# Three transformer blocks in one program: another way to sum the experts, another place for the overflow code, another order of waits at the head

## The chip, the core and the metric

One core of a Trainium2 chip. The time is that of the device for one execution, in microseconds: 2055.23 us, median of 3 runs (2053.47 to 2059.28). TensorE multiplies, ScalarE and VectorE work on rows of up to 128 partitions, GpSimd does small preparations, SyncE issues the stream of weights.

## The reference

Three blocks over 256 tokens of width 1024, all in float32. The one in which most of the change lies is the expert layer of the second block:

```python
logits = xt @ router_w                      # 256 x 8
top_val, top_idx = lax.top_k(logits, 2)
gates = softmax(top_val)
# each token goes to its 2 experts:
y[e] = (silu(x_e @ w1[e]) * (x_e @ w3[e])) @ w2[e]
h = h + sum over the two experts of gate * y[e]
```

Before it come gated linear attention, windowed attention, block attention, differential attention, a dense SwiGLU of width 2816 and a spatial gating unit; behind it a gated embedding layer ("ple"), then the third block (two attentions and a dense SwiGLU) and a last norm.

## The kernel before

All weights of the dense products come in 1 MB chunks (128 x 2048 floats), in the order of use, through a ring of three slots (`stream_part`, two DMAs of half a chunk each). ScalarE rounds each half to a reduced format (`split_high`, L235), VectorE subtracts that from the raw one (`split_low`, L244), and TensorE makes each product from three matmuls, high by high, high by low, low by high (`times`, L259 to L261). A slot of the ring is free when VectorE is through; a slot of the split parts when TensorE is (`used`). ScalarE and VectorE split two chunks ahead of TensorE (`AHEAD`). Everything on an engine runs in program order; there is no planner.

`gated_pe`, `gated_act` and `gated_dve` are the SwiGLU loop for one expert or one dense layer: a turn of the loop takes three chunks, two of up-projection (24 matmuls of 256 columns) and one of down-projection (12 of 512). Each has a hook `between(n)`: n = 0 stands between the two first up-projections, n = 1 before the last down-projection.

The experts run one after the other, each over 128 slots. `route_*` finds the gates and a place for each token in each expert, and a flag `more` that says whether one expert got more than 128 tokens. A 0/1 matrix (`choose`) gathers an expert's tokens by matmul (`gather`, L2575). Before the first expert VectorE also makes 16 matrices of gate-weighted selections (L2665), TensorE transposes them (L2584) and ScalarE copies them to `spread` (L2633). Each expert's sums are copied to `outs` (L2642). At the end TensorE multiplies `spread` by `outs` in plain float32, 32 matmuls, token tile by token tile (L2611), and VectorE adds each quarter to `h` (L2688). Two chunks of zeros follow the experts in the stream, so that what the loop splits ahead is nothing that is used.

Then every engine reads the flag into a register (`overflow`, L2694) and jumps over the code for a second round of experts, which lies in the middle of the program, if the flag is 0, as it is for these inputs. SyncE does the same before it goes on with the stream.

At the head (`block1_*`) all engines wait for three loads issued by ScalarE: the identity, the columns of gains and `gla_down`. TensorE transposes the first half of h's columns (`turn_first`), and in `first_products` waits for all of chunk 0 before it transposes the rest and multiplies. `down_pe` multiplies by `gla_down`'s parts behind that. ScalarE and VectorE meanwhile scale the transposed columns to `xT`, split chunk 0 and 1 and find the norm (`deferred_act`, `scale_h_dve`). The same functions, without the loads, stand at the start of each layer.

## Time and profile before

| what | value |
|---|---|
| median of 3 runs | 2055.23 us |
| the profiled execution | 2054.95 us |
| its span | 2053.5 us |
| TensorE busy | 1941.5 us, 95% |
| VectorE busy | 1399.5 us, 68% |
| ScalarE busy | 1224.5 us, 60% |
| read from memory | 448.95 MB |

The span is the time between the first and last instruction that the profiler saw. PE is TensorE's matmul, PEld its weight load, which overlaps; DVE is VectorE, ACT ScalarE, SP SyncE, POOL GpSimd; a q behind the name is the engine's own queue of control instructions and DMA issues. Matmuls are pipelined, so the length of one in a timeline is longer than the distance to the next. L12 is line 12 of the kernel.

### The profile page before, as it was taken

To read this page: it belongs to the slowest core of one execution; us is meant where nothing else is said; L and a number is where in the kernel's file an instruction comes from. 1 tells how busy PE (TensorE), PEld (TensorE's weight loads), DVE (VectorE), ACT (ScalarE), POOL (GpSimd) and SP (SyncE) were. 2 spreads that over 40 slices of the span, in tenths; PEclk is the share of its full clock that TensorE was granted. 3 is DMA by queue.
4 is the path that set the end of the run, shared out by engine and by line. 5 is a ranking of instruction groups with operands and counts; after the bars stand their busy time and mean duration, and the time that the engine had idled before them with its cause. 6 is when DMAs were issued, how large, how long until landed. Compare 5 with 4: busy or idle time off the path is not lost.

```text
span 2053.5 us, 38415 instructions
## 1 busy us (share of the span) xinstructions
PE 1941.5 (95%) x13371; PEld 1742.7 (85%) x13371; DVE 1399.5 (68%) x2160; ACT 1224.5 (60%) x2091; POOL 48.0 (2%) x85
## 2 busy tenths in 40 slices
PE   7989889899999989999999999999999798999997
PEld 6859789799989878888889888889897697879997
DVE  4565566754556778888888888888886465655445
ACT  6535455444456567777777777777775465445444
POOL 1000000000000000000000000000000021200000
PEclk9979999999999989999999999999999899999999
DMA  7516243455546549898989898989997242225552
GB/s 272 181 62 213 95 141 118 137 182 179 179 145 208 165 148 350 314 343 313 350 308 353 305 345 305 346 314 351 324 344 288 99 158 81 66 86 171 182 178 89
DMA packets 128854, 451.24 MB, mean 220 GB/s; under 512 B 15118, under 2 KB 20142, under 8 KB 128512
## 3 DMA queue, kind: packets, MB, share of 16 engines
q1 hardware_dynamic: 120496, 437.83, 61.7%
q10 hardware_dynamic: 8272, 12.25, 1.8%
q8 instruction: 55, 0.90, 0.2%
q14 instruction: 31, 0.25, 0.0%
HBM read 448.95 MB, written 4.22 MB: 221 GB/s over the span
## 4 chain that ended last, share of the span: by engine, by line
PE 69%; DVE 12%; issue 8%; ACT 8%; DMA 3%; ACTq 0%; DVEq 0%; SPq 0%
PE ps L259 20%; PE ps L260 19%; PE ps L261 19%; DVE low L244 5%; ACT high L235 4%; DMA ring<-in_stream 3%; PE ps L1015 2%; PE ps L998 1%; PE ps L2611 1%; DVE work L745 1%; PE ps L2575 1%; PE ps L393 1%; PE ps L919 1%; PE ps L655 1%; DVE xT_low L2657 1%
## 5 line engine op out<-in xcount | busy, mean ns | idle before, releaser
L244 DVE TENSOR_TENSOR low<-ring,high 128x1024 fp32r<-128x1024 f32 x832 | 984.8, 1222 | 248.4 <-ACT high L235 244.6
L259 PE MATMUL ps<-high,xT_high 128*128 128x256 f32 (+1 forms) x3256 | 961.4, 295 | 24.6 <-DVE xT_low L325 13.2
L235 ACT CAST high<-ring 128x1024 fp32r<-128x1024 f32 x832 | 840.2, 1054 | 180.9 <-PE ps L261 164.2
L260 PE MATMUL ps<-low,xT_high 128*128 128x256 f32 (+1 forms) x3256 | 941.4, 289 | 0.0
L261 PE MATMUL ps<-high,xT_low 128*128 128x256 f32 (+1 forms) x3256 | 937.8, 288 | 0.0
L259 PEld LDWEIGHTS ps<-high,xT_high 128*128 128x128 f32 x3256 | 615.6, 189 | 47.5 <-DVE xT_low L325 15.4
L260 PEld LDWEIGHTS ps<-low,xT_high 128*128 128x128 f32 x3256 | 617.4, 190 | 12.2
L261 PEld LDWEIGHTS ps<-high,xT_low 128*128 128x128 f32 x3256 | 615.5, 189 | 9.7
L259 PE MATMUL ps<-high,smallT_high 128*128 128x512 f32 (+2 forms) x582 | 243.7, 419 | 10.8 <-DVE smallT_low L750 6.2
L261 PE MATMUL ps<-high,smallT_low 128*128 128x512 f32 (+2 forms) x582 | 226.4, 389 | 0.0
L260 PE MATMUL ps<-low,smallT_high 128*128 128x512 f32 (+2 forms) x582 | 225.9, 388 | 0.0
L259 PEld LDWEIGHTS ps<-high,smallT_high 128*128 128x128 f32 (+1 forms) x582 | 110.7, 190 | 61.7 <-DVE smallT_low L750 43.9
L745 DVE TENSOR_TENSOR work<-ps,work 128x128 f32<-128x128 f32 (+1 forms) x220 | 68.4, 311 | 113.4 <-ACT work L707 111.1
L261 PEld LDWEIGHTS ps<-high,smallT_low 128*128 128x128 f32 (+1 forms) x582 | 110.8, 190 | 24.1
L260 PEld LDWEIGHTS ps<-low,smallT_high 128*128 128x128 f32 (+1 forms) x582 | 111.7, 192 | 16.0
L704 ACT ACTIVATE work<-ps 128x128 f32<-128x128 f32 x176 | 49.1, 279 | 112.0 <-PE ps L261 112.0
L707 ACT ACTIVATE work<-ps,small 128x128 f32<-128x128 f32 x88 | 27.6, 364 | 143.0 <-PE ps L261 142.9
L1044 ACT ACTIVATE logit<-logit,small 128x128 f32<-128x128 f32 (+1 forms) x80 | 36.2, 454 | 102.6 <-DVE small L1077 75.7
L655 PE MATMUL ps<-consts,work 128*128 128x128 f32 x264 | 65.0, 274 | 8.7 <-DVE work L745 8.7
L750 DVE TENSOR_TENSOR smallT_low<-ps,smallT_high 128x128 fp32r<-128x128 f32 (+1 forms) x220 | 68.4, 311 | 6.1 <-ACT smallT_high L712 5.2
L712 ACT CAST smallT_high<-ps 128x128 fp32r<-128x128 f32 (+1 forms) x220 | 62.9, 286 | 12.7 <-PE ps L655 7.5
L1222 ACT ACTIVATE proj<-ps,small 128x256 f32<-128x256 f32 x82 | 34.3, 470 | 51.4 <-PE ps L261 51.3
(329 smaller groups left out, 1171.6 us busy)
## 6 DMA issues: line engine op xcount, KB each, us to landing
ring<-in_stream SPq DMA_DIRECT2D x832, 512.0 KB, 5.5
bias_rows<-bias_line ACTq DMA_DIRECT2D x2, 1536.0 KB, 14.3
wide<-in_wide_rows ACTq DMA_DIRECT2D x5, 512.0 KB, 5.4
work<-bias_rows ACTq DMA_DIRECT2D x2, 1024.0 KB, 11.0
h<-in_x SPq DMA_DIRECT2D x2, 512.0 KB, 4.9
work<-bias_rows ACTq DMA_DIRECT2D x2, 512.0 KB, 6.7
consts<-in_consts ACTq DMA_DIRECT2D x1, 869.0 KB
work<-in_p ACTq DMA_DIRECT2D x2, 256.0 KB, 3.2
```

What stands on the lines that cost most here:

```text
L235: A.e.copy(k.high[:, slot, cols], k.ring[:, slot, cols]).then_inc(flow.high_made, 1)
L244: V.e.tensor_tensor(k.low[:, slot, cols], k.ring[:, slot, cols], k.high[:, slot, cols].bitcast(F32), ALU.subtract).then_inc(flow.split, 1)
L259: T.e.matmul(out, x[0], w[0], start=start, stop=False, **more)
L260: T.e.matmul(out, x[0], w[1], start=False, stop=False, **more)
L261: return T.e.matmul(out, x[1], w[0], start=False, stop=stop, **more)
L655: ins = T.e.transpose(ps[:, 6 + f, t * P:(t + 1) * P], act[:, f, t, :], ident)
L704: ins = A.e.activation(silu[:, f, 0:nt, :], hidden[:, f, 0:nt, 0, :], ACT.Silu)
L712: A.e.copy(high[:, f, 0:n], ps[:, 6 + f, 0:n]).then_inc(flow.act_high, 1)
L745: V.e.tensor_tensor(act[:, f, 0:nt, :], hidden[:, f, 0:nt, 1, :], silu[:, f, 0:nt, :], ALU.mult).then_inc(flow.acted, 1)
L750: V.e.tensor_tensor(low[:, f, 0:n], ps[:, 6 + f, 0:n], high[:, f, 0:n].bitcast(F32), ALU.subtract).then_inc(flow.act_low, 1)
L1015: ins = T.e.matmul(out, left, a.values(h, b), start=(b == 0), stop=(b == last))
L1044: ins = A.e.activation(L, L, ACT.Exp, bias=nmax[:, s, t:t + 1], accum_out=total[:, s, t:t + 1])
```

## The change

The eight experts' outputs are no longer summed by gate-weighted float32 matrices. The weighted selections are made, transposed and read only in the last expert: half of them in its first hook, half in its second. ScalarE takes from them each slot's gate (a sum over a row), VectorE a 0/1 selection. Each expert's rows are multiplied by their gates and split into a high and a low part (ScalarE, VectorE) in two alternating places in `xT`, and TensorE multiplies both parts by the 0/1 selection, expert by expert, 64 matmuls in the reduced format, first the columns 0 to 511 of both token tiles, then the others. VectorE adds in the same order, and the transposes of the next layer wait only for the first half. The last expert's rows are read from where TensorE left them, without the copy.

The two chunks of zeros are gone from the stream: the loop now splits the first two chunks of the next layer. The flag is read before the first expert (TensorE) or after it (ScalarE, VectorE) and kept in a register; the code for overflow stands behind the rest of the program, together with a second copy of that rest, and the wait for the stores of the output moved from ScalarE to GpSimd.

At the head TensorE waits for the first half of x, the identity and the gains, not for `gla_down`, and `first_products` transposes before it waits, and waits for half a chunk before the first half of its products. `gla_down` is rounded and its low part made behind the first norm. The zeros for opening banks are made once.

```diff
         self.mix = buf("mix", [P, NT, D])
+        work_at = nc.sbuf_base
         self.work = buf("work", [P, WORK])
+        self.spread = nc.alloc_sbuf_tensor_at("spread", [P, NEXP, SEQ], F32R, offset=work_at + 4 * SPREAD)
         self.logit = buf("logit", [P, 2, NT, KEYS3])
...
         return ins
-    wait_split(T, k.main, c)
-    if sem is not None:
+    if sem is None:
+        T.e.wait_ge(k.s["x_last"], 16)
+        turn_last(T, k, 0)
+        turn_last(T, k, 1)
+    else:
         T.e.wait_ge(sem, T.passed[sem.num] - 1)
-    turn_last(T, k, 0)
+        turn_last(T, k, 0)
+    T.e.wait_ge(k.main.split, 2 * c + 1)
     T.e.wait_ge(parts, T.passed[parts.num])
     products(0, range(4))
     if sem is not None:
         T.e.wait_ge(sem, T.passed[sem.num])
-    turn_last(T, k, 1)
+        turn_last(T, k, 1)
     products(1, range(4))
+    wait_split(T, k.main, c)
...
@@ -513,12 +532,13 @@
     turn_act(A, k, TWO, 4, k.xT[0], gain, at=4)
     if start:
         split_high(A, k, k.main, A.chunk)
-    if sem is not None:
-        A.e.wait_ge(sem, A.passed.get(sem.num, 0) + first)
+    A.e.wait_ge(sem, A.passed.get(sem.num, 0) + first)
     A.step(square_act(A, k, 0))
     preload(A, k, ACT.Sqrt)
     turn_act(A, k, TWO, 4, k.xT[0][:, 4:8, :], gain, at=6, k0=4)
-    if sem is not None:
+    if start:
+        A.e.wait_ge(k.s["x_last"], 16)
+    else:
         A.e.wait_ge(*A.next(sem, last))
     A.join()
     A.tell(square_act(A, k, 1), k.s["squared"])
...
     a, s, e = k.a, k.s, Even(k)
-    A.e.dma_start(k.consts[:, 0:P], a["consts"][:, 0:P]).then_inc(s["first"], 16)
-    A.e.dma_start(k.cols[:, :], a["cols"]).then_inc(s["first"], 16)
-    A.e.dma_start(e.down, a["gla_down"]).then_inc(s["first"], 16)
+    A.e.dma_start(k.consts[:, 0:P], a["consts"][:, 0:P]).then_inc(s["x_first"], 16)
+    A.e.dma_start(k.cols[:, :], a["cols"]).then_inc(s["x_first"], 16)
+    A.e.dma_start(e.down, a["gla_down"]).then_inc(s["down_loaded"], 16)
     A.e.dma_start(k.small[:, 200:202].bitcast(I32), a["positions"]).then_inc(s["params"], 16)
     A.e.dma_start(k.rows[:, :], a["rows"].to_broadcast([P, N_ROWS])).then_inc(s["params"], 16)
...
 def block1_act(A, k):
+    deferred_act(A, k, "norm0", k.s["x_first"], 48, 0, start=True)
+    A.e.wait_ge(k.s["down_loaded"], 16)
     A.tell(A.e.copy(k.smallT[0][:, 0:128], Even(k).down), k.s["down_high"])
-    A.e.wait_ge(k.s["x_last"], 16)
-    deferred_act(A, k, "norm0", None, 0, 0, start=True)
     even_act(A, k)
     deferred_act(A, k, "norm1", k.s["added"], 6, 8)
     load_bias_act(A, k, 0)
@@ -1829,13 +1848,13 @@
 def block1_dve(V, k):
     g = Even(k)
-    V.e.wait_ge(*V.next(k.s["down_high"]))
-    V.tell(V.e.tensor_tensor(k.smallT[1][:, 0:128], g.down, k.smallT[0][:, 0:128].bitcast(F32), ALU.subtract),
-           k.s["down_split"])
     turn_first_dve(V, k, "norm0")
     split_low(V, k, k.main, 0)
     turn_last_dve(V, k, "norm0")
     scale_h_dve(V, k)
+    V.e.wait_ge(*V.next(k.s["down_high"]))
+    V.tell(V.e.tensor_tensor(k.smallT[1][:, 0:128], g.down, k.smallT[0][:, 0:128].bitcast(F32), ALU.subtract),
+           k.s["down_split"])
     split_low(V, k, k.main, 1)
     even_dve(V, k)
...
+def token_sums(k, half, t):
+    return k.ps[:, (4, 5, 0, 1)[2 * half + t], :]
...
+    def turn_weighted(n):
+        T.e.wait_ge(*T.next(flow.weighted))
+        if n:
+            T.e.wait_ge(*T.next(flow.spread_made))
+        for g in range(8):
+            ins = T.e.transpose(ps[:, g // 4, (g % 4) * P:(g % 4 + 1) * P], m.weighted[:, 8 * n + g, :],
+                                k.const("ident"))
+        T.tell(ins, flow.w_turned)
...
-    T.e.wait_ge(*T.next(flow.weighted))
-    for g in range(NEXP * NT):
-        ins = T.e.transpose(ps[:, 4 + g // 4, (g % 4) * P:(g % 4 + 1) * P], m.weighted[:, g, :], k.const("ident"))
-    T.tell(ins, flow.w_turned)
-    T.e.wait_ge(*T.next(flow.spread_made))
-    T.e.wait_ge(*T.next(flow.opened))
+    more = None
+    if read is not None:
+        T.e.wait_ge(*T.next(k.s["routed"]))
+        more = read()
+    T.e.wait_ge(k.s["zero_made"], 1)
...
         def between(n):
+            if n == 0 and e:
+                T.e.wait_ge(flow.kept, kept + e)
             if e == NEXP - 1:
+                turn_weighted(n)
                 return
             if n == 0:
-                if e:
-                    T.e.wait_ge(flow.kept, e)
                 T.e.wait_ge(*T.next(flow.chosen))
...
-    T.e.wait_ge(flow.kept, NEXP)
-    for t in range(NT):
+    T.e.wait_ge(*T.next(flow.spread_made))
+    for e in range(NEXP):
+        T.e.wait_ge(*T.next(flow.part_low))
         for half in range(2):
-            for e in range(NEXP):
-                ins = T.e.matmul(ps[:, 2 * t + half, :], m.spread[:, e, t * P:(t + 1) * P],
-                                 m.outs[:, e * D + half * 512:e * D + (half + 1) * 512],
-                                 start=(e == 0), stop=(e == NEXP - 1))
-            if t == 0 or half == 0:
-                T.tell(ins, flow.combined)
-    ins.then_inc(flow.used, AHEAD)
-    T.e.wait_ge(*T.next(flow.moe_added))
-def moe_act(A, k, flow, c0, u0):
-    m, ps = Moe(k), k.ps
+            for t in range(NT):
+                for n, part in enumerate(out_parts(k, e)):
+                    ins = T.e.matmul(token_sums(k, half, t), m.spread[:, e, t * P:(t + 1) * P],
+                                     part[:, 4 * half:4 * half + 4, :], start=(e == 0 and n == 0),
+                                     stop=(e == NEXP - 1 and n == 1))
+                if e == NEXP - 1:
+                    T.tell(ins, flow.product)
+        if e < NEXP - 2:
+            T.tell(ins, flow.product)
+    return more
...
+    def gates(n):
+        A.e.wait_ge(*A.next(flow.w_turned))
+        for e in range(4):
+            ins = A.e.activation(k.work[:, SCR + e * SEQ:SCR + (e + 1) * SEQ],
+                                 ps[:, e // 2, e % 2 * SEQ:(e % 2 + 1) * SEQ], ACT.Copy,
+                                 accum_out=m.gate[:, 4 * n + e:4 * n + e + 1])
+        if n:
+            A.join()
+        A.tell(ins, flow.gates_made)
+    def rows(e, src):
+        A.tell(A.e.activation(out_parts(k, e)[0], src, ACT.Copy, scale=m.gate[:, e:e + 1]), flow.part_high)
...
-    A.e.wait_ge(*A.next(flow.w_turned))
-    A.tell(A.e.copy(k.work[:, 1280:3328], ps[:, 4:8, :].rearrange("p b w -> p (b w)")), flow.spread_made)
     for e in range(NEXP):
         u = e % 2
         def between(n):
             if e < NEXP - 1:
                 high(1 - u, 2 - 2 * u + n, n)
+                return
+            gates(n)
+            if n == 0:
+                A.e.wait_ge(*A.told(flow.gates_made))
+                rows(0, m.rows(0))
         gated_act(A, k, flow, 1, c0 + e * FFN_CHUNKS, u0 + e, split_high, between)
-        A.e.wait_ge(flow.used, c0 + (e + 1) * FFN_CHUNKS)
-        A.tell(A.e.copy(m.outs[:, e * D:(e + 1) * D], ps[:, 2 * u:2 * u + 2, :].rearrange("p b w -> p (b w)")),
-               flow.kept)
-def moe_dve(V, k, flow, c0, u0, gates, place):
-    m, ps = Moe(k), k.ps
+        if e < NEXP - 1:
+            A.e.wait_ge(flow.used, c0 + (e + 1) * FFN_CHUNKS)
+            A.tell(A.e.copy(m.out(e), ps[:, 2 * u:2 * u + 2, :].rearrange("p b w -> p (b w)")), flow.kept)
+        if e == 0 and read is not None:
+            A.e.wait_ge(*A.next(k.s["routed"]))
+            more = read()
+    A.e.wait_ge(flow.used, c0 + MOE_CHUNKS - 1)
+    A.e.wait_ge(*A.told(flow.gates_made))
+    for e in range(1, NEXP):
+        if e >= 2:
+            A.e.wait_ge(*A.next(flow.product))
+        if e == NEXP - 1:
+            A.e.wait_ge(flow.used, c0 + MOE_CHUNKS)
+        rows(e, m.rows(e) if e < NEXP - 1 else out_sums(k, e))
+    return more
...
+    def weigh(n):
+        for e in range(4 * n, 4 * n + 4):
+            for t in range(NT):
+                ins = V.e.tensor_scalar(m.weighted[:, e * NT + t, :], m.slots, place[:, t, e:e + 1],
+                                        gates[:, t, e:e + 1], ALU.is_equal, ALU.mult)
+        V.tell(ins, flow.weighted)
+    def spread(n):
+        V.e.wait_ge(*V.next(flow.gates_made))
+        for b in range(2):
+            ins = V.e.tensor_scalar(m.spread[:, 4 * n + 2 * b:4 * n + 2 * b + 2, :],
+                                    ps[:, b, :].rearrange("p (e s) -> p e s", e=2), 0.0, None, ALU.is_gt)
+        V.tell(ins, flow.spread_made)
...
+    def rows(e, src):
+        high, low_part = out_parts(k, e)
+        V.e.wait_ge(*V.next(flow.part_high))
+        V.tell(V.e.scalar_tensor_tensor(low_part, src, m.gate[:, e:e + 1], high.bitcast(F32), ALU.mult, ALU.subtract),
+               flow.part_low)
...
-    make_zero(V, k, flow)
     for e in range(NEXP):
         u = e % 2
         if e < NEXP - 1:
-            V.e.wait_ge(flow.gathered, 2 * (e + 1))
+            V.e.wait_ge(flow.product, product + 2 * (e + 1))
             choose(e + 1)
         def between(n):
             if e < NEXP - 1:
                 low(1 - u, 2 - 2 * u + n, n)
+            else:
+                spread(n)
+            if (e, n) == (NEXP - 2, 1):
+                weigh(0)
+            if (e, n) == (NEXP - 1, 0):
+                weigh(1)
+                rows(0, m.rows(0))
...
-    for t in range(NT):
-        for half in range(2):
-            if t == 0 or half == 0:
-                V.e.wait_ge(*V.next(flow.combined))
-            else:
-                V.e.wait_ge(flow.used, c0 + MOE_CHUNKS + AHEAD)
-            cols = slice(half * 512, (half + 1) * 512)
-            ins = V.e.tensor_tensor(k.h[:, t, cols], k.h[:, t, cols], ps[:, 2 * t + half, :], ALU.add)
-    V.tell(ins, flow.moe_added)
+        if e == 0 and read is not None:
+            V.e.wait_ge(*V.told(k.s["routed"]))
+            more = read()
+    for e in range(1, NEXP):
+        rows(e, m.rows(e) if e < NEXP - 1 else out_sums(k, e))
+    return more
+def moe_add_dve(V, k, turn):
+    for half in range(2):
+        cols = slice(half * 512, (half + 1) * 512)
+        for t in range(NT):
+            V.e.wait_ge(k.main.product, turn * (3 * NEXP + 2) + 3 * NEXP - 2 + 2 * half + t + 1)
+            V.tell(V.e.tensor_tensor(k.h[:, t, cols], k.h[:, t, cols], token_sums(k, half, t), ALU.add),
+                   k.main.moe_added)
...
+def after_experts_pe(T, k):
+    T.e.wait_ge(*T.next(k.main.moe_added, 2))
+    turn_first(T, k)
+    T.next(k.s["parts_low"], 2)
+    T.next(k.main.moe_added, 2)
+    ple_pe(T, k, k.main.moe_added)
...
+def after_experts_dve(V, k):
+    moe_add_dve(V, k, 1 if V.again else 0)
+    turn_first_dve(V, k, "ple1")
+    turn_last_dve(V, k, "ple1")
+    scale_h_dve(V, k)
+    ple_dve(V, k, "third")
+    scale_twice_dve(V, k)
...
-    T.e.wait_ge(k.s["first"], 48)
     block1_pe(T, k)
-    block2_pe(T, k)
-    block3_pe(T, k)
+    more = block2_pe(T, k)
+    over = T.other_way()
+    with k.nc.If(more == 0):
+        after_experts_pe(T, k)
+        block3_pe(T, k)
+    with k.nc.Else():
+        moe_again_pe(over, k)
+        after_experts_pe(over, k)
+        block3_pe(over, k)
...
-        sp.wait_ge(k.again.split, 2 * (MOE_CHUNKS + AHEAD))
-    stream_part(k, k.main, part, k.n_chunks, 0)
-    sp.wait_ge(k.s["final_done"], 1)
-    sp.dma_start(k.out.rearrange("b (t p) d -> p (b t) d", p=P)[:, 0, :], k.h[:, 0, :]).then_inc(k.s["out_stored"], 16)
+    more = overflow(k, ENG.SP)
+    with k.nc.If(more == 0):
+        stream_part(k, k.main, part, k.n_chunks, 0)
+        store_rows_sync(k)
+    with k.nc.Else():
+        stream_part(k, k.main, k.moe_at, k.n_chunks, -AHEAD - MOE_CHUNKS)
+        store_rows_sync(k)
...
+    G.e.wait_ge(k.s["out_stored"], 32)
...
-        swiglu(w["moe_w1_2"][0], w["moe_w3_2"][0], w["moe_w2_2"][0]), np.zeros((AHEAD, P, CHUNK), np.float32),
+        swiglu(w["moe_w1_2"][0], w["moe_w3_2"][0], w["moe_w2_2"][0]),
```

## Rows read from the trace of the kernel before

**Rows 1.** windows: span and length, busy time of each engine (instructions), granted clock, DMA share, GB/s

```profile
1507.10:1516.20 9.10, 9.00 (x64) 8.11 (x64) 7.91 (x11) 6.81 (x11) 0.00 (x0) 1.00 1.00 370
```

**Rows 2.** chain that ended last: start, length, what; the experts' sums and after

```profile
1578.83 27.75 PE ps L2611 x64
...
1607.30 4.57 issue
```

**Rows 3.** DMA issues: count, size of one, median us from issue to landing

```profile
ring<-in_stream SPq DMA_DIRECT2D x7, 512.0 KB, 9.2
...
h<-in_x SPq DMA_DIRECT2D x2, 512.0 KB, 4.9
...
out<-h ACTq DMA_DIRECT2D x1, 512.0 KB, 3.6
```

**Rows 4.** timeline of the head: start, length, engine, what, idle before it and its releaser

```profile
6.41 1.28 ACT L1819 ACT_TABLE_LOAD   x1 [6.41 <-issue]
...
8.40 1.97 PE L393 MATMUL ps<-consts,h 128*128 128x128 f32 x8 [8.40 <-DMA proj<-in_gla_down]
...
14.71 1.08 PE L393 MATMUL ps<-consts,h 128*128 128x128 f32 x4 [4.35 <-DVE low L244]
...
23.67 0.28 PE L259 MATMUL ps<-xT_high,smallT_high 128*16 128x256 f32 x1
```

**Rows 5.** windows, columns as in rows 1: TensorE's clock in four stretches

```profile
14.70:19.60 4.90, 4.88 (x23) 4.90 (x24) 0.00 (x0) 1.93 (x5) 0.73 (x3) 1.00 1.02 415
...
19.60:24.00 4.40, 4.40 (x38) 4.33 (x37) 3.57 (x12) 3.97 (x10) 3.38 (x13) 1.00 0.21 82
...
740.00:743.50 3.50, 3.50 (x19) 3.50 (x18) 1.98 (x2) 1.82 (x2) 0.00 (x0) 0.52 0.34 111
...
1612.00:1624.00 12.00, 7.74 (x36) 7.34 (x37) 4.98 (x9) 8.04 (x17) 0.00 (x0) 0.50 0.38 134
```

**Rows 6.** timeline of the experts' opening

```profile
736.21 1.13 DVE L2657 SCALAR_TENSOR_TENSOR xT_low<-ps,cols,xT_high 128x128 fp32r<-128x128 f32 x4 [0.85 <-ACT xT_high L2626]
...
738.70 0.70 PE L786 MATMUL ps<-nought 1*128 1x512 f32 x2 [1.96 <-ACT work L2633]
```

**Rows 7.** instructions of L2694, L393, L673: shortest/median/longest ns, first and last start

```profile
L2694 PEldq TENSOR_LOAD <-work x1: 484/484/484, 1607.3 to 1607.3; - x1
...
L393 PEldq COMPARE_BRANCH  x1: 3623/3623/3623, 1608.2 to 1608.2; - x1
...
L673 PEldq COMPARE_BRANCH  x100: 76/215/237, 434.7 to 2034.2; - x100
```

**Rows 8.** last expert's opening: VectorE's and TensorE's timelines, then instructions of L2439, L2665

```profile
1478.15 2.36 DVE L244 TENSOR_TENSOR low<-ring,high 128x1024 fp32r<-128x1024 f32 x2 [1.95 <-ACT high L235]
...
1481.28 2.36 DVE L244 TENSOR_TENSOR low<-ring,high 128x1024 fp32r<-128x1024 f32 x2 [0.56 <-ACT high L235]
...
1485.63 0.48 PE L259 MATMUL ps<-high,smallT_high 128*128 128x512 f32 x1
...
1488.59 0.28 PE L259 MATMUL ps<-high,xT_high 128*128 128x256 f32 x1
...
L2439 ACT ACTIVATE proj<-ps,cols x4: 467/472/477, 713.7 to 719.7; 128x256 f32<-128x256 f32 x4
...
L2665 DVE TENSOR_SCALAR proj<-consts,work x16: 335/337/339, 729.0 to 732.9; 128x128 f32<-128x128 f32 x16
```

**Rows 9.** costliest groups: busy us, mean ns; the last row as in rows 7

```profile
L244 DVE TENSOR_TENSOR low<-ring,high 128x1024 fp32r<-128x1024 f32 x832 | 984.8, 1222 | 248.4 <-ACT high L235 244.6
...
L235 ACT CAST high<-ring 128x1024 fp32r<-128x1024 f32 x832 | 840.2, 1054 | 180.9 <-PE ps L261 164.2
...
L2688 DVE TENSOR_TENSOR h<-h,ps x4: 689/689/689, 1586.0 to 1606.6; 128x512 f32<-128x512 f32 x4
```

**Rows 10.** timeline behind the experts

```profile
1618.10 1.11 PE L393 MATMUL ps<-consts,h 128*128 128x128 f32 x4 [4.26 <-DVE low L244]
...
1629.04 0.38 PE L259 MATMUL ps<-high,xT_high 128*128 128x256 f32 x1 [0.99 <-DVE low L244]
```

213 lines of the change are left out of this document (117 added, 96 removed).

## The prediction

> **What bounds the kernel now.** I read the windows of the stages first, then the chain of waits, then the timelines around each place of the diff. In the experts' loop TensorE is the bound: in 9.1 us, the time of one turn, it is busy 9.00 us at the full clock, VectorE 7.91 us, the DMA queues all the time [rows 1]. So an edit pays only where TensorE stands still or does avoidable work, and VectorE has just 1.2 us of slack a turn. The chain names two such places in one stretch: 27.75 us of sums over the experts (L2611) and 4.57 us of "issue" behind them [rows 2]. The head of the program and the opening of the experts are the others.
>
> **Head (gain 2.9).** TensorE's first transposes start at 8.40, released by the gla_down load; the products wait again for VectorE's low parts (4.35 us idle, transposes 14.71) [rows 4]. Now the start waits for the first half of x (the first issue of SyncE, median 4.9 to land [rows 3]; I allow until 6.2) and for the identity and the gains, small loads issued by ScalarE ahead of gla_down. ScalarE is then the later one: its table load ends at 7.69 [rows 4]. So its four xT_high run from 7.7 to 9.4, the two splits of chunk 0 from 9.4 to 11.4 (its halves land some 6.7 and 8 us after issue at 1.8 and 2.3, an estimate from the median 9.2 of seven issues [rows 3]), and the first low half is ready at 11.7. TensorE, with all transposes done, starts products at 11.8. The profile's clock row says 1.00 there, but TensorE issued 23 matmuls in 4.9 us and then 38 in 4.4 us: 0.213 against 0.116 us each, half and full clock [rows 5]. 24 products at 0.213 end at 16.9; the low parts of the last columns are there by 16.9 (ScalarE: squares, table load, four xT_high to 15.9); the other 24 at 0.116 end at 19.8, 3.8 sooner. But the down products, which followed at 23.67 before [rows 4], now wait for gla_down's parts, which ScalarE copies only after the squares and the splits of chunk 1: 15.9 + 1.4 squares + 0.8 variance and root + 1.9 splits + 0.3 = 20.3, and VectorE's part 0.3 later. They start at 20.8: 2.9 of the 3.8 us survive. Bounds: 1.5 (x late, chunk 0 late) to 3.8 (the down parts hidden).
>
> **Opening of the experts (gain 1.3).** Gone are 16 transposes and a 1.87 us copy, behind which TensorE opened the banks at 738.70. The token parts were complete at 736.21 + 1.13 = 737.34 [rows 6]; now that is what ends last. The early read of the flag is a load of 0.48 us on TensorE, some 0.9 us with the register work up to the branch [rows 7]; it lies in TensorE's gap before 737.4. ScalarE's and VectorE's reads fall behind expert 0, where VectorE waits some 1.9 us, as before expert 7 [rows 8], and TensorE has 16 gathers to do: nothing, at most 1 us. Bounds 0 to 1.3.
>
> **Last expert's opening (loss 6.1).** This is the step that speaks against the change. VectorE weighs the first half of the selections (8 x 0.26, pitch from 4.18 us for 16; the row's 337 ns is latency) behind expert 6, in a wait of 1.95 us [rows 8]: free. Behind the first activation of expert 7 it waits for ScalarE's four copies with sums (4 x 0.47 = 1.9 [rows 8]; ScalarE starts them at 1480.95, when TensorE's 8 transposes are done), then makes 0/1 from two banks (2 x 0.67), weighs eight more (2.1) and makes the low parts of expert 0's rows (1.22 [rows 9]): 1482.85 + 1.35 + 2.1 + 1.2 = 1487.5. Its split of the next chunk stood at 1481.28 [rows 8]. It is 6.2 us late in a loop in which it needs 7.9 of 9.1 us [rows 1]. TensorE's down products began at 1485.63 and ended at 1488.59 (12 in 2.96 us, 0.24 each) [rows 8]; they need VectorE's activation, then its low parts, then one more chunk of 2.3 us: the second six now start at 1493.2, not 1487.1. TensorE can't win that back, having no slack. Bounds: 3 (the slack of its first turn absorbs half) and 8 (the chunk ring falls behind as well).
>
> **Tail (gain 20.6).** All in the old time. 8 more transposes put off the last down products by 0.8: end 78.4 of 1500. ScalarE does the next chunk's splits to 76.9, the second four copies to 78.6, VectorE the second selections to 80.1. From there on TensorE sums: per expert 8 matmuls of 512 columns, 8 x 0.24 = 1.9 us, 15.2 in all, against 32 four-byte ones of 0.87 us. Two slots alternate, so a slot's round is ScalarE 1.05, VectorE 1.22 [rows 9], TensorE 1.9 and some 0.3 of signals = 4.5 us for two experts. Three rounds behind the first pair (80.2 to 84.0, rounds start 80.2, 84.7, 89.3, 93.8) end the sums at 97.6. Column half 0 of both token tiles is there at 96.8, its two adds (0.69 each [rows 9]) at 97.8, and TensorE turns there; it turned at 1611.87 before: 14.1 earlier. In that are the branch, 3.62 us on TensorE [rows 7], which becomes fall-through, and the adds.
>
> The Trainium skill, "Runtime: NRT & Kernel Launch", section "Instruction fetch mechanics", says that prefetch is sequential and that a taken branch out of the window fetches its page first. The trace agrees: 3.62 us for the far one, 0.215 for those of the loop.
>
> The zero chunks go, so the next real chunks are split already inside the last expert. Before, the products began after transposes at 1618.10, released by VectorE's split, at the half clock (granted 0.50 [rows 5]). Now low parts end last: ScalarE 98.5 to 100.0, VectorE to 101.1 (1500s), products from 1601.1; 24 at full clock and the turn between them 3.2 us, then the low parts of columns 512 on (ScalarE until 1604.6, VectorE until 1605.6), 24 more: 1607.7. The chunk after it began at 1629.04, 0.99 us late on its split [rows 10]; now that one is split too: 1608.4. Gain 20.6. Bounds: 12 (half clock through the sums: 8 x 1.5 us, less what the rounds hide) and 23.
>
> **Rest (0).** The final program must jump over the other way's code: at most 3.6 us, but ScalarE's store takes 3.6 us to land anyway [rows 3], and the wait for it moved to GpSimd, which does not jump. In the other layers no transposes waited on a split, so the new order of first_products gives nothing.
>
> Sum: 2.9 + 1.3 - 6.1 + 20.6 = 18.7. The profiled execution took 2054.95 us (span 2053.5), 0.3 under the median 2055.23: 2054.95 - 18.7 = 2036.3.
>
> **Rivals.** (A) As above, 70%: 2032 to 2041.
> (B) VectorE's burst is hidden (the chunks split ahead cover it): then only TensorE's 8 transposes stay of the 6.1 (0.9), 2031. For it: two chunks are split ahead. Against: the activation behind the burst isn't. 7%.
> (C) The clock falls in the sums, whose TensorE share is 1.9 of 2.25 and which begin behind a wait of 1.7 us; after the 1.96 us wait at 738.70 [rows 6] it fell to 0.52 for 740.0 to 743.5 [rows 5]. Then an expert takes 8 x 0.43 = 3.4 us: 27.4 in place of 17.5, and the next products lose 3 more: 2036.3 + 9.9 + 3 = 2049. Against: the gaps between rounds are 0.7 us, a third of the one that preceded that fall. With half of that, 2043. 12%.
> (D) The change doesn't do what it says: the no-overflow way still takes a far branch. 3.6 more: 2040. 6%.
> (E) Slower. The double buffer of parts doesn't work: each expert's sum waits for its own ScalarE and VectorE steps and runs at the half clock: 8 x (1.05 + 1.22 + 3.4 + 0.4) = 48.6 instead of 17.5, and 3 us for cold products: 2070. It decides from 35 us of sums on. Against: the waits of slots are by e - 2. 2%.
> (F) The gain is given back in the layers behind (the chunk stream, freed earlier, meets the loads of bias and weights): 3 to 8 us, 2043. For it: nothing in the rows but that DMA was idle there before. 3%.
>
> Forecast 2036.3. Range 2031 to 2045: all of A, B's, D, and half of C and F. No change is within 0.3% (6 us), what a measurement of this kernel can tell: 2049 to 2061, part of C and the unforeseen: 3%. Slower 2%, faster 95%.
>
> **What would show it.** Right: first product near 11.8 and down products near 20.8; TensorE idle some 3.5 and 1.4 us in the first turn of expert 7 behind VectorE; sums of 17 to 18 us with gaps of 0.7; no 3.6 us branch; product of the next layer at full clock 1 to 2 us behind the adds. Wrong: a granted clock of 0.5 in the sums, a TensorE that doesn't wait in expert 7, or a turn of the later layers that is longer than before.

## Result, and the profile after

The changed kernel took 2035.62 us (median of 4 executions, 2032.45 to 2038.16) against 2054.51 us of the kernel before (median of 4). The medians differ by 18.9 us. The ratio over the executions is 0.9903, with a 95% interval of 0.9881 to 0.9925, which is 19.9 us, or 1.0%, faster. The forecast was 2036.3, within 2031 to 2045. The profiled execution took 2036.76 us with a span of 2034.9, which is 18.6 us less than the span before.

How well can the total be known? The kernel before, run a second time with nothing edited, gave 2054.73 us (median of 12, 2049.78 to 2059.53) and a ratio of 0.9997 [0.9987, 1.0008]. Single executions of one kernel lie up to 12 us apart (2048.16 to 2060.29 beside again). So a step of 1 to 4 us is read in the traces at its own place, and hardly in the total.

**The head.** The timelines of the changed kernel's first 12 us, of TensorE, ScalarE and VectorE, answer to [rows 4]:

```profile
5.33 0.47 PE L407 MATMUL ps<-consts,h 128*128 128x128 f32 x1 [5.33 <-DMA cols<-in_cols]
...
6.65 1.28 ACT L327 ACT_TABLE_LOAD   x1 [6.65 <-PE ps L407]
7.94 1.57 ACT L327 ACTIVATE xT_high<-ps,cols 128x256 fp32r<-128x256 f32 x4
...
8.81 1.66 DVE L339 SCALAR_TENSOR_TENSOR xT_low<-ps,cols,xT_high 128x256 fp32r<-128x256 f32 x4 [3.19 <-ACT xT_high L327]
10.48 2.36 DVE L258 TENSOR_TENSOR low<-ring,high 128x1024 fp32r<-128x1024 f32 x2
...
11.76 0.58 PE L273 MATMUL ps<-high,xT_high 128*128 128x256 f32 x1 [2.75 <-DVE low L258]
```

The transposes wait for the gains' load in place of gla_down's, and the first product starts at 11.76 (forecast 11.8), where TensorE before was still idle.

**The last expert's opening.** First ScalarE and VectorE, then TensorE, in the first turn of expert 7 (before: [rows 8]); the last row is the window of a clock fall inside it, with columns as in [rows 1]:

```profile
1479.17 0.38 ACT L2687 ACTIVATE work<-ps 128x256 f32<-128x256 f32 x1 [0.60 <-PE ps L2625]
...
1480.77 1.29 DVE L2748 TENSOR_SCALAR spread<-ps 128x512 fp32r<-128x512 f32 x2 [1.77 <-ACT work L2687]
1481.98 2.14 DVE L2740 TENSOR_SCALAR work<-consts,work 128x128 f32<-128x128 f32 x8
1484.03 1.28 DVE L2763 SCALAR_TENSOR_TENSOR xT_low<-proj,small,xT_high 128x1024 fp32r<-128x1024 f32 x1
1485.23 2.35 DVE L258 TENSOR_TENSOR low<-ring,high 128x1024 fp32r<-128x1024 f32 x2
1487.50 0.28 DVE L765 TENSOR_TENSOR work<-ps,work 128x128 f32<-128x128 f32 x1
...
1487.84 0.33 PE L675 MATMUL ps<-consts,work 128*128 128x128 f32 x1 [2.90 <-DVE work L765]
...
1488.20:1491.60 3.40, 3.40 (x8) 2.35 (x9) 3.40 (x5) 2.16 (x3) 0.00 (x0) 0.52 0.98 266
```

VectorE stands in one unbroken queue from 1480.77 on: comparisons, weighing, rows, split, and only then the activation that TensorE has waited for since 1484.9.

**The sums and the next layer.** TensorE's rounds, VectorE's adds, the products of the next layer (before: [rows 2, 10]), then the window of the sums:

```profile
1582.97 0.50 PE L2663 MATMUL ps<-xT_high,spread 128*128 128x512 f32 x1 [1.36 <-DVE spread L2748]
1587.70 0.50 PE L2663 MATMUL ps<-xT_high,spread 128*128 128x512 f32 x1 [0.65 <-DVE xT_low L2763]
...
1597.11 0.50 PE L2663 MATMUL ps<-xT_high,spread 128*128 128x512 f32 x1 [0.65 <-DVE xT_low L2763]
...
1599.78 2.48 DVE L2800 TENSOR_TENSOR h<-h,ps 128x512 f32<-128x512 f32 x4 [0.85 <-PE ps L2663]
...
1601.12 1.53 PE L407 MATMUL ps<-consts,h 128*128 128x128 f32 x12
...
1604.49 0.36 PE L273 MATMUL ps<-high,xT_high 128*128 128x256 f32 x1 [1.84 <-DVE xT_low L339]
1608.31 0.36 PE L273 MATMUL ps<-high,xT_high 128*128 128x256 f32 x1 [0.30 <-DVE xT_low L339]
...
1583.00:1601.00 18.00, 16.08 (x64) 11.60 (x64) 10.11 (x10) 6.88 (x6) 0.00 (x0) 1.00 0.21 73
```

Eight experts are summed in 18.0 us at the full clock, in rounds 4.7 us apart, with gaps of 0.65.

**Branches, the flag and the end.** Instructions by line as in [rows 7], DMA issues as in [rows 3]:

```profile
L2806 PEldq TENSOR_LOAD <-work x1: 489/489/489, 730.6 to 730.6; - x1
...
L3431 PEldq COMPARE_BRANCH  x2: 83/1690/3296, 1599.0 to 2023.4; - x2
...
out<-h SPq DMA_DIRECT2D x1, 512.0 KB, 3.0
out<-h ACTq DMA_DIRECT2D x1, 512.0 KB, 4.5
```

The branch behind the sums costs 83 ns and is not far; the far one, 3.3 us, now stands at TensorE's end. ScalarE's last store takes 4.5 us to land, not 3.6.

**The ledger.** The word half-clock phase stands below for a stretch in which the profile shows TensorE's granted clock at 0.5, which is 1.2 instead of 2.4 GHz. The same branches of TensorE's chunk loops (L673 in [rows 7]) serve as marks in all kernels, since each has the same 13371 matmuls in its trace. Each row gives the length of a stretch in us. The first chunk of the next layer's second group (1629.04 in [rows 10]) is the 2787th matmul from the end in all of them.

```
stretch                                  before  before2  after   again
start to first chunk loop                434.68  436.31   433.05  431.74
... to its 10th turn                     156.60  156.60   156.60  156.60
... to expert 0's 2nd turn               173.53  172.87   172.59  171.84
... to expert 6's last turn              703.32  702.70   704.15  703.90
expert 7's opening (to its 1st turn)      21.29   21.31    27.10   28.04
expert 7's turns                          81.91   81.91    81.03   81.32
sums, up to the next layer's 2nd chunk    57.72   57.14    37.05   38.14
... to the last layer's first turn       248.53  250.67   246.41  244.86
the last layer's turns                   156.59  156.63   156.60  156.63
last turn to end                          19.32   20.83    20.31   20.25
```

### The profile page after: what moved, and what is told of

Its sections match the earlier page's. It is cut to its first block, busy times and chain, and to the rows that moved or that the text cites. A ratio compares the mean times of both kernels' runs of the same rounds, so it can differ in the third digit from the quotient of the medians.

```text
span 2034.9 us, 38437 instructions
## 1 busy us (share of the span) xinstructions
PE 1923.6 (95%) x13371; PEld 1737.1 (85%) x13371; DVE 1407.2 (69%) x2166; ACT 1228.4 (60%) x2109; POOL 50.3 (2%) x85
## 4 chain that ended last, share of the span: by engine, by line
PE 73%; DVE 11%; ACT 7%; issue 6%; DMA 2%; ACTq 1%; DVEq 0%; SPq 0%
PE ps L273 22%; PE ps L274 21%; PE ps L275 21%; DVE low L258 4%; ACT high L249 3%; PE ps L1034 2%; DMA ring<-in_stream 2%; PE ps L1017 1%; PE ps L675 1%; PE ps L2616 1%; DVE xT_low L339 1%; PE ps L938 1%; DVE xT_low L2755 1%; DVE work L765 1%; PE ps L1045 1%
```

## The experiments

**again and before2: what an unchanged kernel does.** Nothing was edited.

> The changed kernel once more, nothing edited. Theory: the 1.6 us that are left of the head's 3.8 us gain at 434 us is a matter of where the half-clock phases fall, which differs from execution to execution; so another execution of the same code loses or keeps a different part of it: the head itself is the same to 0.1 us up to 98 us (first product at 11.8, 3.8 us ahead of the kernel before), the ledger behind it moves by up to 2 us, and so does the end. Rival: the earlier head drags its stream into a fixed collision (a transfer or a buffer) at 104, 175 and 295 us; then the ledger between 98 and 434 us is the same as in the first profile to 0.2 us. Ratio to before 0.990 by both.

> The kernel before, once more, nothing edited: a second profile of it, and what the comparison makes of no difference (ratio 1.000, interval about 0.002 to each side). Theory (what differs beyond the forecast steps is where the half-clock phases fall): the places of the steps keep their times to 0.2 us (first product, the last expert's opening 21.3 us, 57.7 us from the last turn of expert 7 to the second chunk of the next layer, or 1.1 more with a half-clock phase in it), while the stretches without an edit, up to 434 us and from the next layer's second chunk to the last layer (248.5 us), differ by 1 to 3 us from the first profile. Rival (the change made these stretches shorter too, by its chunk stream): the second profile of before has 248.5 us there to 0.3.

again: 2035.80 us (median of 6), ratio 0.9903 [0.9883, 0.9922]. The matmul that before starts at 97 us is 3.57 us ahead here, the one at 118 us 2.98 (first profile: 3.76, then 3.02), so this loss occurred again; but then this run keeps 2.93 to 434 us, where the first profile fell to 1.63. The early loss is no fixed collision either. In the five profiles with a half-clock phase of 6.8 us that starts at 99 us (after, again, hook, hooklate, weighlate) the lead falls by 0.6 to 0.8 us between these two matmuls; in the six others with the new head, whose phases lie elsewhere, it changes by -0.1 to +0.4. The later loss goes with a phase between 290 and 297 us: of the six profiles with the new head that have one, five lose 1.4 to 2.2 us from 200 to 300 us (weighlate doesn't), and the five without lose at most 0.1. So the theory holds, and the rival of a fixed collision falls. Over all eleven profiles with the new head, the first loop is reached at 430.2 to 433.1, on average at 431.7 us; with the old one (before, before2, oldhead) at 434.7, 436.3 and 436.1. The gain is thus some 4.0 us on average and not the 1.6 that one pair of profiles shows.

before2's stretch from the next layer's second chunk to the last layer took 250.67 us, not 248.53 to 0.3: the rival as I had put it (the change shortened this stretch) falls. Its length goes with the clock. The windows of that stretch, in turn of before, before2 and again:

```profile
1629.04:1877.58 248.54, 234.50 (x1627) 204.05 (x1628) 152.27 (x318) 131.00 (x288) 38.23 (x56) 0.95 0.35 113
```

```profile
1628.83:1879.50 250.67, 236.61 (x1627) 205.48 (x1627) 152.20 (x318) 131.11 (x288) 38.22 (x56) 0.94 0.35 112
```

```profile
1611.58:1856.44 244.86, 230.69 (x1630) 201.41 (x1628) 151.58 (x317) 130.60 (x288) 38.24 (x56) 0.97 0.34 110
```

The same work, the same other engines; TensorE's clock is 0.95, 0.94 and 0.97. Kernels with the changed tail can be long there too: oldhead 248.86, weighlate2 248.58, oneslot 249.48 and weighlate 250.76 us, with 24 to 31 us at half clock, where the eight others have 17 us of it and 244.9 to 246.9. Whether the change makes the short form more frequent, two profiles of before can't tell. The tail's own stretch differed by 0.6 us between the two profiles of before, a little outside what I had written.

**oldhead: the head's waits as before.** All of the head's part of the change is undone, and with it the new order of first_products.

```
-    T.e.wait_ge(k.s["x_first"], 48)
+    T.e.wait_ge(k.s["x_first"], 16)
...
-    deferred_act(A, k, "norm0", k.s["x_first"], 48, 0, start=True)
-    A.e.wait_ge(k.s["down_loaded"], 16)
     A.tell(A.e.copy(k.smallT[0][:, 0:128], Even(k).down), k.s["down_high"])
+    A.e.wait_ge(k.s["x_last"], 16)
+    deferred_act(A, k, "norm0", None, 0, 0, start=True)
...
+    T.e.wait_ge(k.s["first"], 48)
```

> The changed kernel with the head's waits as they were before (TensorE, ScalarE and VectorE wait for all first loads again), all else as changed. Theory: the head starts 3.8 us later up to 98 us; in the median over many executions the loss at the end lies between 1.6 us (what the first profile kept) and 3.8 us: ratio to before 0.9914 to 0.9925 against 0.9903. Rival (the head's gain is always given back before the experts, by a wait further on): the end moves under 0.5 us, ratio to before 0.9905 or less.

At 97 us it is 0.21 us behind the kernel before, and it reaches the first loop at 436.13. The time, 2037.64 us (median of 6) and a ratio of 0.9912 [0.9891, 0.9934], is 1.8 us above again's on the same chip, inside the theory's 1.6 to 3.8; the ratio is just short of its 0.9914, though, and the intervals overlap, so only the marks show the loss: 3.8 us at 97 us (the eleven with the new head are 3.24 to 3.79 ahead of before there, 3.6 on average), and 4.4 us at the first loop, against their average.

**hook: nothing in the last expert's first hook.** Both halves are turned, copied and compared in the second hook (into four banks), the first rows too, and the weighing stands behind experts 5 and 6.

```
             if e == NEXP - 1:
-                turn_weighted(n)
+                if n:
+                    turn_weighted(0)
+                    turn_weighted(1)
                 return
...
+            if (e, n) == (NEXP - 3, 1):
+                weigh(0)
             if (e, n) == (NEXP - 2, 1):
-                weigh(0)
-            if (e, n) == (NEXP - 1, 0):
                 weigh(1)
-                rows(0, m.rows(0))
```

> The changed kernel with all that was put into the first hook of the last expert's opening (turning half of the weighted selections, their copies on ScalarE, the comparisons and weighing on VectorE, the first rows) moved to the second hook of the same expert, and the weighing itself behind experts 5 and 6. Theory: the 5.8 us that the last expert's opening lost are VectorE's and ScalarE's queues ahead of the down product (TensorE waited 2.9 us for VectorE at 1487.84); without this work in that place they go. The selections for the sums come later then, since both halves are turned in one hook: I price that at 2.6 us later sums. In sum 3.2 us faster than the changed kernel, about 2032.4 us, ratio to before 0.9888. Rival (the loss is the half-clock phase at 1488.1 to 1491.5, which has its own time): the opening keeps 2 us or more of its loss, and the end is the same as the changed kernel's or up to 2.6 us later.

2035.34 us (median of 6), 0.9904 [0.9887, 0.9921]: no gain in the total. The theory's first part holds: the opening takes 21.58 us, against 27.10. VectorE's timeline there has its order of before again:

```profile
1477.85 2.36 DVE L258 TENSOR_TENSOR low<-ring,high 128x1024 fp32r<-128x1024 f32 x2 [0.55 <-ACT high L249]
1480.12 0.29 DVE L765 TENSOR_TENSOR work<-ps,work 128x128 f32<-128x128 f32 x1
```

But the turns behind it take 82.63 us instead of 81.03, and from the last turn to the next layer's second chunk it is 42.42 instead of 37.05. The sums wait 3.42 us for a queue of eight copies and four comparisons, and then their first round, the products of two experts, lasts 6.11 us instead of 4.73:

```profile
1580.28 0.56 PE L2663 MATMUL ps<-xT_high,spread 128*128 128x512 f32 x1 [3.42 <-DVE xT_low L2765]
...
1586.39 0.50 PE L2663 MATMUL ps<-xT_high,spread 128*128 128x512 f32 x1 [0.59 <-DVE xT_low L2765]
```

The clock record has a phase of 3.4 us at half clock from 1580.5 on, 0.2 us behind the start of the sums. So the 5.4 us of this stretch are three things: the sums start 11.37 us after the last turn and not 8.44, which is 2.9 us where I had priced 2.6; the half-clock phase in them costs 1.4; and one in the next layer's first products, at 1604.4, costs 1.1 (see weigh). Of the 5.5 us won in the first hook 1.6 go into the turns, which I had at nothing, and 2.9 into the second hook; the rest is lost to the two phases of this execution. Why a turn takes 9.17 us here, 9.10 in before and 9.00 in the changed kernel, no run shows.

**hooklate: hook and late (below) together.**

```
-        gated_act(A, k, flow, 1, c0 + e * FFN_CHUNKS, u0 + e, split_high, between)
+        gated_act(A, k, flow, 1, c0 + e * FFN_CHUNKS, u0 + e, split_high if e < NEXP - 1 else all_but(
+            split_high, c0 + MOE_CHUNKS + 1), between)
```

> As hook, and also the split of the second chunk of the next layer's weights (ScalarE's high part, VectorE's low part) moved from the last expert to behind the sums. Theory: VectorE reaches the comparisons for the sums 2.3 us earlier (its split took that at 1579.22 to 1581.6), so the sums start about 2.2 us earlier than in hook; the split is hidden beside TensorE's turning of the next layer. About 5.4 us faster than the changed kernel, ratio to before 0.9877. Rival (the sums then wait for ScalarE's rows or the turned selections instead, or the next layer's product waits for the late split): no faster than hook, or up to 1 us slower.

2033.36 us (median of 6), 0.9895 [0.9876, 0.9913]. The opening again takes 21.58 us, the turns 82.56, and from the last turn to the second chunk 39.81, 2.6 us less than in hook. Only 1.2 of that is the late split: the sums start 10.18 us after the last turn, where hook's start at 11.37, and 2.2 were expected. The other 1.4 are hook's half-clock phase in the sums, which this execution doesn't have. Against the changed kernel the three stretches together gain 1.2 us, or 2.3 without the half-clock phase that fell into the last one, not 5.4: the turns were longer (1.5) and the late split brought 1.0 less than expected, besides 0.3 each for the opening and the second hook.

**weigh: only the weighing moved.**

```
-            if (e, n) == (NEXP - 2, 1):
+            if (e, n) == (NEXP - 3, 1):
                 weigh(0)
-            if (e, n) == (NEXP - 1, 0):
+            if (e, n) == (NEXP - 2, 1):
                 weigh(1)
+            if (e, n) == (NEXP - 1, 0):
                 rows(0, m.rows(0))
```

> The changed kernel with only the weighing moved: VectorE weighs the first half behind expert 5 and the second half behind expert 6, instead of behind expert 6 and in the first hook of expert 7. All else stays in that hook. Theory (each instruction ahead of the down product on VectorE costs its own time there): eight weighings are 2.1 us of VectorE's queue, so expert 7's opening, which took 27.1 us from the last turn of expert 6 to the first of expert 7 (21.3 before), takes 25.0; the sums behind it keep their length, so the end is 2.1 us earlier. Rival (ScalarE's copies or the half clock set that opening): 26.5 to 28.

The opening takes 25.39 us. In seven kernels that left it alone it took 26.65 to 28.04, 27.2 on average. TensorE's wait of 2.90 has become two of 0.85 and 0.93:

```profile
1482.01 0.33 PE L675 MATMUL ps<-consts,work 128*128 128x128 f32 x1 [0.85 <-DVE work L765]
1484.87 0.50 PE L273 MATMUL ps<-high,smallT_high 128*128 128x512 f32 x1 [0.93 <-DVE smallT_low L770]
```

The time is 2031.87 us (median of 4), 0.9895 [0.9877, 0.9912]. That is 3.8 us under the changed kernel's median, more than the opening explains; the intervals overlap.

The seven also show the clock's share. Without a half-clock phase in the opening (one run, whole) it took 26.65 us, with 3.4 us at half clock 26.84 to 27.34, with 6.8 us (again) 28.04. Thus 5.3 us of the loss stand without it, and the rival of a clock fall explains 0.2 to 1.4. The three profiles with the weighing moved (this one, 24.65 and 24.61 below) had none either: against 26.65 they gain 1.3 to 2.0 us, of the 2.1 that VectorE weighs. In the next layer's first products such a phase cost 1.1 us (again: 38.14 to the second chunk, against 37.05; weigh 38.25).

**late: the second chunk of the next layer split behind the sums.**

```
+    split_high(A, k, flow, c0 + MOE_CHUNKS + 1)      (end of moe_act)
...
     turn_first_dve(V, k, "ple1")
+    split_low(V, k, k.main, V.chunk + 1)             (after_experts_dve)
```

> The changed kernel with the split of the second chunk of the next layer's weights moved from the last expert to behind the sums. Theory: VectorE, whose comparisons for the sums stand behind this split (2.3 us), lets the sums start 1.9 us earlier; the stretch from the last turn of expert 7 to the branch behind the sums, 24.5 us, becomes 22.6, and the next layer takes the split beside TensorE's products. Rival: the products of the next layer wait for the late split, and what the sums gain is lost by the next layer's first loop.

The branch behind the sums comes 23.30 us after the last turn, not 24.49: 1.2 us, where 1.9 were expected. TensorE's wait ahead of the sums was only 1.36 us long, and 0.18 of it is left:

```profile
1577.17 0.50 PE L2670 MATMUL ps<-xT_high,spread 128*128 128x512 f32 x1 [0.18 <-DVE spread L2757]
```

That is all there was to win: TensorE itself is busy with its last down products until 1576.99, and VectorE's comparisons, which end at 1577.12, now wait 1.89 us for ScalarE's copies of the turned selections. The next layer didn't wait for the late split: from TensorE's turning to the second chunk it took 11.5 us, as in again, which has the same half-clock phase there; the rival falls. The time is 2032.87 us (median of 4), 0.9903 [0.9880, 0.9927].

**weighlate and weighlate2: both.** The two diffs above.

> weigh and late together, in one place each. Theory: the two gains add, 4.0 us faster than the changed kernel (25.0 us for the opening, 22.6 us from the last turn to the branch), ratio to before 0.9884. Rival (moving all of the first hook, as in hook, showed that the turns that follow become longer, 9.17 instead of 9.00 us, and took 1.6 us back): the turns of expert 7 go back to 9.1 us or more when VectorE is less late in them, and 0.9 us or more of the gain goes.

> weighlate once more, for more executions beside those of the first call. Theory: 3 us faster than the changed kernel in the median, ratio to before 0.9885 to 0.989. Rival (the two gains are lost in the spread of the half-clock phases): a ratio within 0.0005 of the changed kernel's 0.9903.

The opening takes 24.65 and 24.61 us, the turns 81.20 and 81.02 (they do not grow longer; that rival falls), the stretch to the second chunk 36.34 and 35.89 instead of 37.05. 2032.33 us (median of 5) at 0.9885 [0.9868, 0.9901], and 2033.91 (median of 4) at 0.9899 [0.9884, 0.9915]. The nine executions of both have a median of 2032.8; the ten of the changed kernel have 2035.8. That is 3 us, where opening (against the average of 27.2) and last stretch together show 3.2 to 3.7; but the intervals of the two ratios overlap, so by the total alone it isn't shown that this version beats the changed one. Nor is it shown that it beats weigh alone (2031.87).

**far: the two ways exchanged.** On all four engines, for example:

```
-    with k.nc.If(more == 0):
-        after_experts_pe(T, k)
-        block3_pe(T, k)
-    with k.nc.Else():
+    with k.nc.If(more > 0):
         moe_again_pe(over, k)
...
+    with k.nc.Else():
+        after_experts_pe(T, k)
+        block3_pe(T, k)
```

> The changed kernel with the two ways behind the experts exchanged: the code for overflow lies next, the common way behind it, so that each engine takes the far branch. Theory: TensorE, which comes to the branch 2.1 us before the adds let it go on, takes the 3.6 us that this branch took before, so the next layer starts 1.5 us later, and the end is 1.5 us later. Rival (the full price is on the path, since ScalarE and VectorE pay it too): 3.6 us later.

2037.19 us (median of 4), 0.9917 [0.9900, 0.9934]. Three rows of it, the branch, TensorE's turning of the next layer, and the last store:

```profile
L3432 PEldq COMPARE_BRANCH  x1: 3591/3591/3591, 1594.9 to 1594.9; - x1
...
1598.59 1.53 PE L407 MATMUL ps<-consts,h 128*128 128x128 f32 x12 [1.53 <-DVE h L2800]
...
out<-h ACTq DMA_DIRECT2D x1, 512.0 KB, 3.6
```

The turning comes 28.15 us after the last turn (1570.44), against 26.60: 1.55 us, as in the theory. The store row was not in it: where the common way lies last and no engine jumps at its end, ScalarE's store lands in 3.6 us as before.

**oneslot: no double buffer in the sums.**

```
-        if e >= 2:
-            A.e.wait_ge(*A.next(flow.product))
+        A.e.wait_ge(*A.next(flow.product))
```

> The changed kernel with one edit: before ScalarE makes the rows of an expert in the sums it waits for TensorE's sum of the expert just before, not of the one before that, so that the two slots no longer overlap. Theory: each expert then takes ScalarE 1.15, VectorE 1.28, TensorE 1.9 and about 0.4 us of signals one after the other, 4.7 us, instead of 2.25: the sums take 7 x 4.7 + 1.9 = 35 us instead of 18, 17 us more, if TensorE keeps its full clock through gaps of 2.8 us; at half clock an expert takes 6.6 us and the sums 50, 32 us more. Rival (the rounds were set by something else, so that the slots matter little): under 5 us more.

Rounds of one expert, then the window from the first to the last:

```profile
1582.01 0.51 PE L2663 MATMUL ps<-xT_high,spread 128*128 128x512 f32 x1 [1.36 <-DVE spread L2747]
1586.80 0.80 PE L2663 MATMUL ps<-xT_high,spread 128*128 128x512 f32 x1 [2.64 <-DVE xT_low L2762]
...
1622.70 0.50 PE L2663 MATMUL ps<-xT_high,spread 128*128 128x512 f32 x1 [2.52 <-DVE xT_low L2762]
...
1582.01:1622.70 40.69, 22.72 (x56) 15.05 (x56) 9.00 (x7) 8.00 (x7) 0.00 (x0) 0.71 0.10 32
```

An expert takes 40.69 / 7 = 5.8 us, between my two ends of 4.7 and 6.6, since the clock falls for part of the time (granted 0.71). Its first fall, at 1586.4, lies in the first gap of 2.64 us. From the last turn to the second chunk it is 62.60 us, 25.5 more. Without the two slots the tail is 4.9 us longer than before (57.72), and the whole kernel takes 2066.01 us (one execution), beside 2054.60 of before.

**whole: all adds wait for the last sum.**

```
-            V.e.wait_ge(k.main.product, ... + 2 * half + t + 1)
+            V.e.wait_ge(k.main.product, ... + 4)
```

> The changed kernel with VectorE's four adds waiting for the last of the sums, so that the order by column halves brings nothing. Theory: the first half is there four matmuls of 0.24 us ahead of the second, so the adds, and with them TensorE's turning and the next layer, come 1.0 us later. Rival (the next layer's start hangs on ScalarE's and VectorE's parts of the last columns, which the halves don't move): under 0.3 us.

The rival falls. The one execution took 2034.55 us. The turning comes 28.04 us after the last turn, 1.44 later than in the changed kernel, and the second chunk 1.46. I had counted four matmuls ahead of the end; the first add needs only token tile 0 of its half, which is six matmuls ahead: 6 x 0.24 = 1.44.

## Why the prediction was right

The steps as the marks show them, in us:

```
step                          forecast   measured
head                           +2.9      +3.6 (at 97 us, eleven profiles; 3.2 to 3.8)
experts' opening               +1.3      +1.7 (173.2 - 171.5, 2 and 12 profiles)
last expert's opening          -6.1      -5.9 (27.2 against 21.3)
its later turns                 0        +0.8 (0.9 and 0.6)
tail                          +20.6      +20.7 (57.72 - 37.05; before2 - again: 19.0)
end                             0        -1.0
sum                           +18.7      +19.9; by the ratio 0.9903 also 19.9
```

**Head: mechanism right, size 0.7 too small.** The first product came when forecast, and all of the 3.8 us that I had counted for the products survived (3.76 in the first profile). The step that failed is the next one, that the down products would hold up 0.9 of it: ScalarE's xT_high, squares, root and splits together were 0.8 us faster than I had added them up. Its copy of gla_down ended at 19.50 and VectorE's part at 19.83, not 20.3 and 20.6, and the down products followed the others without a wait at 19.93.

**Experts' opening.** 1.3 was the upper bound, and the average of the profiles is 1.7; with half-clock phases between 715 and 744 us in every one of them and a spread of 2.5 us among the new ones (170.1 to 172.6), the difference isn't resolved. This stretch begins at 591 us, and a half-clock phase at 593 to 597 us, in before and five of the others, alone makes it 1.5 us longer. From the matmul that starts at 700 us in before to the opening of the banks it is 38.64 and 39.47 us in before and before2, 38.35 in oldhead with as much time at half clock as before, and 38.2 in the five with as much as before2: 0.3 and 1.3 us. The flag's early read on TensorE (0.489 us at 730.6) lies beside the last gathers, which keep their pace, ahead of a wait of 2.49 us. The reads on VectorE and ScalarE (841.2 and 842.5) cost nothing: the marks on either side of them, expert 0's last turn and expert 1's first, are 2.83 and 2.84 us ahead of before.

**Last expert.** The queue came as written. TensorE waited 2.90 us for VectorE's activation (forecast 3.5), and its second six down products began at 1490.70, where 1493.2 in the old time is 1491.5 in this profile's. The second wait (forecast 1.4) is missing here, where TensorE went through the first six at half clock; in whole, with the full clock in the opening, the two waits are 2.90 and 0.93. hook gave back 5.5 us of it, weigh 1.3 to 2.0 of the weighing's 2.1: the cause is shown. "TensorE can't win that back" was too strict: the later turns took 9.00 instead of 9.10 us.

**Tail.** Measured from expert 7's last turn (1571.33 before, 1574.52 after), in forecast and in fact: sums start 8.9 and 8.45, turning 26.5 and 26.6, products 29.8 and 29.97, second chunk 37.1 and 37.05. Of the 20.7 us, 14.0 are won up to the turning (40.5 us after the last turn before, 26.6 now) and 6.7 behind it (17.2 and 10.5). The 6.7 have two causes that no run separates: the first chunks are split earlier, and TensorE's granted clock there is 1.00 (before: 0.64 from 1611.80 to 1629.04). Nor did a run keep the float32 sums in the new order, so the share of the reduced format in the 14.0 isn't measured by itself. Rival C, a fall of the clock in the sums, did not come in the changed kernel (granted 1.00, gaps of 0.65), but two variants had it: oneslot, with gaps of 2.6, and hook, whose sums begin behind a wait of 3.42 instead of 1.36 us; hook had 3.4 us of it at their start and lost 1.4 us by it. Where a half-clock phase fell into the next layer's first products (again, weigh, late, far) 1.1 us more were needed. Rival E, priced at 2070, is oneslot: 2066, at half clock for part of the time only.

The rule of the Trainium skill that the prediction cited ("Runtime: NRT & Kernel Launch", section "Instruction fetch mechanics") held in both directions: fall-through 83 ns, taken far branches 3.3 us at the end of the changed kernel (3.3 to 3.8 in the eleven that take it) and 3.6 in far. On the path of the new order it is worth only 1.5 us (far), because TensorE waits for the adds there anyhow; Rival D, the far branch still taken, was priced at the full 3.6 and would have been this 1.5.

**End: the step "rest 0" failed.** I had the far jump's 3.6 us hidden behind the store, and it is (TensorE's ends at 2026.7). But the store itself takes 0.9 us longer. In the eleven kernels with a jump behind the common way its store landed in 4.2 to 4.6 us; in before, before2 and far, which have none, in 3.6. Windows of the fourth microsecond behind the store's issue show it, of the changed kernel and then of far:

```profile
2033.32:2034.32 1.00, 0.00 (x0) 0.00 (x0) 0.00 (x0) 0.00 (x0) 0.00 (x0) 0.50 0.15 53
```

```profile
2032.25:2033.25 1.00, 0.00 (x0) 0.00 (x0) 0.00 (x0) 0.00 (x0) 0.00 (x0) 0.50 0.03 8
```

In far all but nothing moves any more, in the changed kernel the store's bytes still do. That the order of the ways decides it is shown. The traces also show what runs beside the store: the jumps of ScalarE, SyncE and VectorE are each taken within 1.2 us of its issue, and between 0.2 us ahead of this issue and 3.7 us behind it (2030.2 to 2034.0 in the changed kernel) each of the eleven has four packets of 8 KB on an instruction queue; before, before2 and far have none there. The store's slowest packet takes 0.31 us instead of 0.18, and its last one ends 3.7 us behind the issue, not 3.2, in all eleven. So fetching of code beside the store is seen, and half of the 0.9 us is in the store's own packets. That the fetch delays them wasn't tried by moving one jump alone, and the other half, between the last packet and the landing, is open.

The total missed by 1.2 us by these marks: head +0.7, opening +0.4, turns +0.8, last expert +0.2 and tail +0.1, less 1.0 at the end. So part of its accuracy is errors of both signs that cancel. The rows of the table are not of one pair of profiles, and by the other pair the tail is 19.0, so that they agree with the ratio's 19.9 is in part chance; by the medians the gain is 18.9.

## What to carry to other kernels

Work put into a hook of a loop costs what it takes on the engine whose next result the bound engine waits for, and moving it to another hook moves most of the price (hook: 5.5 us won, 4.5 given back); it is free only where that engine waits (weigh). In a chain of three engines over many small steps ask first what the second buffer hides: here 25 us, more than the tail gained. Compare two profiles mark by mark and take several of each: two executions of one kernel had 1.6 us between them at 434 us and 2.1 in a later stretch of 250, as much as most single edits bring. Lay the clock record beside every stretch that is compared: more than half of what the late split seemed to bring between hook and hooklate (1.4 of 2.6 us) was a half-clock phase in one of the two.

## What I had not expected of the hardware

A store at the end of the program lands 0.9 us later (4.5 instead of 3.6 us for 512 KB) in the kernels whose engines take far branches within 1.2 us of its issue; packets of an instruction queue run beside it there, and the store's own packets take up to 0.31 instead of 0.18 us.

Half-clock phases come at other places from execution to execution of the same code, and each costs by what TensorE has to do in it: 3.4 us of it in the last expert's opening 0.2 to 0.7 us, in the next layer's first products 1.1 us, at the start of hook's sums 1.4 us.
